# The convolution's four query channels during the projections, the other eight inside the attention heads

## The reference, cut to what matters

```python
def causal_conv(u, prev, w):                  # u: the 12 GDN channels, prompt: prev = 0
    full = jnp.concatenate([prev, u], axis=1)
    out = full[:, 0:L] * w[0]
    for i in range(1, CONV_W):                # CONV_W = 4
        out = out + full[:, i:i + L] * w[i]
    return out, full[:, L:]                   # the last three raw columns are an output
# gdn_mix: c = silu(out); q, k, v = split(c); q = l2norm(q) * 128**-0.5; k = l2norm(k); chunked delta rule
```

## Time and profile before

| | |
|---|---|
| time, median of 3 runs | 2565.94 us (2563.76 to 2568.59) |
| the profiled execution | 2564.64 us, of which its span is 2562.8 us |
| PE busy | 2469.6 us (96%) |
| weight load on PE busy | 2377.6 us (93%) |
| DVE busy | 1271.2 us (50%) |
| ACT busy | 563.2 us (22%) |
| POOL busy | 1692.2 us (66%) |
| mean granted clock of TensorE | 0.984 of full speed |

### The profile page before, as it was taken

The page is one execution under the profiler, slowest core; times in us unless marked ns, Lnnn a source line. Parts: engine busy times, 40 slices in busy tenths (PEclk is TensorE's granted clock), DMA queues, the critical chain, the costliest instruction groups (busy, mean ns, idle before and its releaser), DMA issues.

```text
span 2562.8 us, 52697 instructions
## 1 busy us (share of the span) xinstructions
PE 2469.6 (96%) x20031; PEld 2377.6 (93%) x20031; DVE 1271.2 (50%) x2204; ACT 563.2 (22%) x851; POOL 1692.2 (66%) x753
## 2 busy tenths in 40 slices
PE   7999998998799999999999999999999899999997
PEld 7999998997577899999999999999999799999996
DVE  4444435787533644443344443367767544444433
ACT  3222101003834222220022220122232211222101
POOL 5777776673523577777777787765555377777773
PEclk9999999998899999999999999999999999999998
DMA  4333333896466333333333333324333333333331
GB/s 120 92 92 95 100 91 77 273 313 193 139 199 190 103 91 90 90 99 91 106 91 90 91 99 90 89 86 124 121 94 119 102 95 88 92 95 90 100 92 56
DMA packets 472550, 291.20 MB, mean 114 GB/s; under 512 B 32945, under 2 KB 438571, under 8 KB 472430
## 3 DMA queue, kind: packets, MB, share of 16 engines
q1 hardware_dynamic: 415510, 235.83, 31.4%
q10 hardware_dynamic: 56928, 53.86, 6.5%
HBM read 273.50 MB, written 16.23 MB: 113 GB/s over the span
## 4 chain that ended last, share of the span: by engine, by line
PE 87%; DVE 7%; ACT 3%; POOL 1%; issue 1%; DMA 0%; ACTq 0%; SPq 0%; DVEq 0%; POOLq 0%
PE ACC L835 76%; PE ACC L1103 2%; PE ACC L1072 1%; POOL WLO L727 1%; PE ACC L1371 1%; PE ACC L1381 1%; DVE TB L2377 1%; DVE RMOL L2316 0%; PE ACC L1383 0%; POOL WHI L724 0%; DVE XL L1835 0%; DVE SSR L2294 0%; PE ACC L1282 0%; PE ACC L1168 0%; PE ACC L929 0%
## 5 line engine op out<-in xcount | busy, mean ns | idle before, releaser
L724 POOL TENSOR_TENSOR WHI<-RAW,ZERO 128x1024 fp32r<-128x1024 f32 (+1 forms) x341 | 691.5, 2028 | 635.7 <-PE ACC L835 593.1
L727 POOL TENSOR_TENSOR WLO<-RAW,WHI 128x1024 fp32r<-128x1024 f32 (+1 forms) x341 | 914.9, 2683 | 48.0
L835 PE MATMUL ACC<-XH,WHI 128*128 128x260 f32 x4032 | 821.9, 285 | 4.2 <-DVE XL L1835 1.9
L835 PE MATMUL ACC<-XH,WLO 128*128 128x260 f32 x4032 | 813.0, 283 | 0.0
L835 PE MATMUL ACC<-XL,WHI 128*128 128x260 f32 x4032 | 811.2, 283 | 0.0
L835 PEld LDWEIGHTS ACC<-XH,WHI 128*128 128x128 f32 x4032 | 624.2, 189 | 22.9 <-DVE PRJ L1922 6.1
L835 PEld LDWEIGHTS ACC<-XH,WLO 128*128 128x128 f32 x4032 | 622.0, 189 | 0.0
L835 PEld LDWEIGHTS ACC<-XL,WHI 128*128 128x128 f32 x4032 | 620.8, 188 | 0.0
L835 PE MATMUL ACC<-HH,WHI 128*128 128x260 f32 x1408 | 284.1, 283 | 1.1 <-POOL WLO L727 1.1
L835 PE MATMUL ACC<-HH,WLO 128*128 128x260 f32 x1408 | 283.1, 282 | 0.0
L835 PE MATMUL ACC<-HL,WHI 128*128 128x260 f32 x1408 | 282.5, 282 | 0.0
(11 more groups left out here) (403 smaller groups left out, 2368.7 us busy)
## 6 DMA issues: line engine op xcount, KB each, us to landing
RAW<-in_ffn_w_gu SPq DMA_DIRECT2D x176, 512.0 KB, 3.9
RAW<-in_ffn_w_down SPq DMA_DIRECT2D x64, 704.0 KB, 4.7
KPAGES<-in_cache_fox_k ACTq DMA_DIRECT2D x128, 256.0 KB, 4.3
VPAGES<-in_cache_fox_v SPq DMA_DIRECT2D x128, 256.0 KB, 3.7
RAW<-in_c_w_in SPq DMA_DIRECT2D x48, 512.0 KB, 3.9
RAW<-in_ab_w_in SPq DMA_DIRECT2D x28, 512.0 KB, 4.9
SSR<-in_state_ret_S ACTq DMA_DIRECT2D x8, 1024.0 KB, 6.8
out<-SSR ACTq DMA_DIRECT2D x8, 1024.0 KB, 5.6
```

The lines of the kernel that those rows point to most:

```text
L724: pool.tensor_tensor(WHI[:, slot, 0:nk, :], RAW[:, slot, 0:nk, :], ZERO[:, :].broadcast_to([P, nk, P]), ALU.add).then_inc(hi_split, 1)
L727: pool.tensor_tensor(WLO[:, slot, 0:nk, :], RAW[:, slot, 0:nk, :], WHI[:, slot, 0:nk, :].bitcast(F32), ALU.subtract).then_inc(split, 1)
L835: ins = pe.matmul(ACC[acc][:, n, 0:HALF], w[:, slot, k, :], a[:, k0 + k, n * HALF:(n + 1) * HALF], start=first and opens, stop=final and c ...
```

## The change: which channels are convolved where

Channels 0 to 3 are convolved during the projections. On ACT one step of `early_tap` (one shifted copy, or the scaling) follows each of the key loads 14 to 29; five buffers are taken in turn (SQ, SSQ, TB, TA and a new TAPX). The raw last columns are first copied to RAWTAIL, from which PE turns them. On POOL one addition (`early_add`) follows the split of each of the channels 18 to 27, and two more follow after those. Channels 4 to 11 go into the heads: 4, 5, 6 in head 0 at A, B and C; 7, 8, 9 in head 1, of which 7 and 8 both stand at B (A is empty) and 9 at C; 10 and 11 in head 2 at B and C (A is empty). None is left in the normalising.

```diff
+        EARLY_CONV, EARLY_BATCH = 4, 14
+        RAWTAIL = new("RAWTAIL", [P, EARLY_CONV, DEC + CONV_W - 1], area="ab")
+        EARLY_TAPS = (SQ, SSQ, TB, TA, at("TAPX", ...))
 POOL
-            split_phase("ab_in", KD, AB_CH // 4, 4, skip=1)
+            first_taps = AB_CONV + EARLY_CONV + 2
+            with pool.Fori(0, AB_CONV // 4) as i:
+                for s in range(4):
+                    split_unit(AB_UNIT + 4 * i + s, (AB_UNIT + s) % 2, KD, 2 * i + (AB_UNIT + s) // 2 + 1)
+
+            def early_add(n):
+                c, shift = n // (CONV_W - 1), n % (CONV_W - 1) + 1
+                pool.wait_ge(cv_tap, c + 1)
+                if shift > 1:
+                    await_step(pool, cv_pool, f"add{shift - 1}", c)
+                out = PRJ[:, AB_CONV + c, shift:SEQ]
+                cv_pool.done(pool.tensor_tensor(out, out, EARLY_TAPS[n % len(EARLY_TAPS)][:, shift:SEQ], ALU.add), f"add{shift}")
+
+            for f in range(AB_CONV, AB_CH):
+                split_unit(AB_UNIT + f, (AB_UNIT + f) % 2, KD, (AB_UNIT + f) // 2 + 1)
+                if f >= first_taps:
+                    early_add(f - first_taps)
+            for n in range(AB_CH - first_taps, EARLY_CONV * (CONV_W - 1)):
+                early_add(n)
...
             convolve_samples()
-            for c in range(CONV_CH):
+            for c in range(EARLY_CONV, CONV_CH):
                 convolve(c)
 PE
+            pe.wait_ge(cv_shifted, EARLY_CONV)
             for c in range(CONV_CH):
...
+                raw = RAWTAIL[:, c, :] if c < EARLY_CONV else PRJ[:, AB_CONV + c, SEQ - CONV_W + 1:TOK]
 ACT
+            def early_tap(c, k):
+                source = PRJ[:, AB_CONV + c, :]
+                if k == 0:
+                    act.wait_ge(tile_free, AB_TILE + AB_CONV + c + 5)
+                    act.activation(RAWTAIL[:, c, :], source[:, SEQ - CONV_W + 1:TOK], ACT.Copy)
+                if k < CONV_W - 1:
+                    shift, n = k + 1, (CONV_W - 1) * c + k
+                    if n == 3:
+                        act.wait_ge(gate_dve.sem, gate_dve.value("gcs"))
+                    if n >= len(EARLY_TAPS):
+                        reader = n - len(EARLY_TAPS)
+                        await_step(act, cv_pool, f"add{reader % (CONV_W - 1) + 1}", reader // (CONV_W - 1))
+                    ins = act.activation(EARLY_TAPS[n % len(EARLY_TAPS)][:, shift:SEQ], source[:, 0:SEQ - shift], ACT.Copy, scale=...)
...
+                else:
+                    act.wait_ge(cv_shifted, c + 1)
+                    act.activation(source[:, 0:SEQ], source[:, 0:SEQ], ACT.Copy, scale=...).then_inc(cv_tap, 1)
             for n in range(KEY_BATCHES):
                 load_keys(act, n % K_SLOTS, KBATCH * n, n)
+                if 0 <= n - EARLY_BATCH < EARLY_CONV * CONV_W:
+                    early_tap((n - EARLY_BATCH) // CONV_W, (n - EARLY_BATCH) % CONV_W)
...
             def conv_taps(c):
-                if c == 0:
+                if c == EARLY_CONV:
                     act.wait_ge(gp_pe.sem, gp_pe.value("tails"))
-                if c >= 2:
-                    await_step(act, cv_pool, "add3", c - 2)
+                await_step(act, cv_pool, "add3", max(c - 2, EARLY_CONV - 1))
...
                 if not last:
-                    conv_taps(3 * h)
+                    if h == 0:
+                        conv_taps(EARLY_CONV)
                     fox_turned(h, 2)
                     exponent(h + 1, 0)
                     exponent(h + 1, 1)
-                    conv_taps(3 * h + 1)
+                    if h == 1:
+                        conv_taps(EARLY_CONV + 3)
+                    conv_taps(EARLY_CONV + (1, 4, 6)[h])
                     fox_turned(h, 3)
                     exponent(h + 1, 2)
-                    conv_taps(3 * h + 2)
+                    conv_taps(EARLY_CONV + (2, 5, 7)[h])
...
-            for c in range(3 * (FOX_HEADS - 1), CONV_CH):
-                conv_taps(c)
```

More of the change, by code:

```diff
@@ L427, in trunk_program @@
         cs_pool = Steps(sem("cs_pool"), ["m0", "m1", "a1", "m2", "a2", "m3", "a3"])
+        EARLY_CONV, EARLY_BATCH = 4, 14
+        RAWTAIL = new("RAWTAIL", [P, EARLY_CONV, DEC + CONV_W - 1], area="ab")
+        EARLY_TAPS = (SQ, SSQ, TB, TA, at("TAPX", [P, SEQ], mo_at + PAGES_BYTES * K_SLOTS // 2 + 4 * CONV_CH * P))
         CONV_TILES = ((SQ, SSQ, TH), [at(f"TAP{n}", [P, SEQ], mo_at + 4 * (KD + FOX_HEADS) * TOK + 4 * SEQ * n) for n in range(3)])
@@ L1020, in _ @@
             pe.wait_ge(gp_act.sem, gp_act.value("prev"))
+            pe.wait_ge(cv_shifted, EARLY_CONV)
             for c in range(CONV_CH):
-                ins = pe.transpose(bank((2, 3, 6)[c // 4])[0:DEC + CONV_W - 1, (c % 4) * P:(c % 4 + 1) * P],
-                                   PRJ[:, AB_CONV + c, SEQ - CONV_W + 1:TOK], IDENT[:, :])
+                raw = RAWTAIL[:, c, :] if c < EARLY_CONV else PRJ[:, AB_CONV + c, SEQ - CONV_W + 1:TOK]
+                ins = pe.transpose(bank((2, 3, 6)[c // 4])[0:DEC + CONV_W - 1, (c % 4) * P:(c % 4 + 1) * P], raw, IDENT[:, :])
             gp_pe.done(ins, "tails")
@@ L1515, in _ @@
             act.wait_ge(pt_in, 48)
+            def early_tap(c, k):
[10 more added lines that the diff above has]
+                        await_step(act, cv_pool, f"add{reader % (CONV_W - 1) + 1}", reader // (CONV_W - 1))
+                    tap = PAR_CONV + CONV_CH * (CONV_W - 1 - shift) + c
+                    ins = act.activation(EARLY_TAPS[n % len(EARLY_TAPS)][:, shift:SEQ], source[:, 0:SEQ - shift], ACT.Copy, scale=PAR[:, tap:tap + 1])
+                    if k == CONV_W - 2:
+                        ins.then_inc(cv_shifted, 1)
+                else:
+                    act.wait_ge(cv_shifted, c + 1)
+                    tap = PAR_CONV + CONV_CH * (CONV_W - 1) + c
+                    act.activation(source[:, 0:SEQ], source[:, 0:SEQ], ACT.Copy, scale=PAR[:, tap:tap + 1]).then_inc(cv_tap, 1)
             for n in range(KEY_BATCHES):
                 load_keys(act, n % K_SLOTS, KBATCH * n, n)
+                if 0 <= n - EARLY_BATCH < EARLY_CONV * CONV_W:
+                    early_tap((n - EARLY_BATCH) // CONV_W, (n - EARLY_BATCH) % CONV_W)
             def channels(first, count):
@@ L1558, in _ @@
             fox_query(0)
+            await_step(act, cv_pool, "add3", EARLY_CONV - 2)
             fox_keys(0)
@@ L2009, in fox_value_tokens @@
                 await_step(dve, fa_pe, "vtok", h)
+                if h == 0:
+                    await_step(dve, cv_pool, "add3", EARLY_CONV - 2)
                 if h >= 2:
```

## The result

The changed kernel takes 2570.21 us, median of 19 runs (2564.64 to 2576.31), and the kernel before 2566.34 us (2562.85 to 2570.87, 19 runs): ratio 1.0014 [1.0007, 1.002], which is 3.6 us more (the medians themselves are 3.9 us apart), and inside the 0.2% that I had called "same". The interval excludes 1, so the sign is real. The profiled execution of the changed kernel has a span of 2567.8 us at a mean granted clock of 0.982; that of before 2562.8 us at 0.984.

A forecast was written before the change was run, and what follows sets the result against it. PE bounds the projections, ACT fills the heads, and PE's spreads and DVE's products carry the normalising. Terms 0 + 0 + 2.5 + 0 + 0 = +2.5 us on the 2565.94 us median gave 2568.4 us, range 2562.5 to 2572.0.

The forecast's parts named there:

- Head 1, +2.5 us: Head 1: A empty and 7, 8 both at B make ACT wait for PE, DVE and POOL; head ends 2.5 us later.
- Head 2, nothing given back: Head 2: the channel removed from A becomes ACT idle time, as key copy, PE and DVE set the exponential; 0 us.
- Projections, 0: Projections: four channels' work on ACT and POOL is hidden under PE; 0 us, bounds 0 to 1.5 us.
- The margin that I had worked out for late weights: Projections, channel 23's split: low part ends 567.49, PE needs it at 567.83, 0.34 us of margin.
- Head 0, 0: Head 0: A, B and C hold one channel each as before, no earlier channel pending; 0 us.
- Normalising, 0, and BEGE: Normalising: three channels off the chain leave, 0 us; BEGE's 0.80 us may shrink, bounds 0 to -0.7, absorbed waiting for PE.
- ACT's amount of work: Rival, heads: ACT's work sets the pace, nine channels becoming eight gives 2.6 us, 2563.3 us; chance 0.17.
- POOL's lateness: Rival, projections: loads 1.5 us late in three units, PE stands still 4 us, 2572.4 us; chance 0.11.
- The clock: Third rival, head 2: idle PE runs one more stretch at its lower clock, 2 us on top, 2570.4 us; chance 0.11.

The follow-up runs named there:

- Number 1: Changed kernel with channel 7 back at A of head 1, 8 at B and 9 at C: 2565.67 us against 2565.9, ratio 0.9999.
- number 8: The changed kernel run again, unaltered, for a second profile: 2569.45 us, ratio 1.0015 to the kernel before.
- Number 4: Changed kernel with channels 7, 8, 9 at A, B, C of head 1, 10 and 11 at A and B of head 2: 2566.12 us, ratio 1.0002.
- number 7: Changed kernel with all three channels of head 1 (7, 8, 9) at B, C empty: 2571.17 us, ratio 1.0022.
- 2: Changed kernel with 7 and 8 at B and C of head 1, 9 and 10 in head 2, 11 in the normalising: 2566.44 us, ratio 1.0002.
- number 5: The light version without the early convolution work of channels 0 to 3 (only the raw-column copy stays): 2562.36 us, ratio 0.9988.
- 3 second run: The light version made again on a different chip run: 2562.70 us against 2565.75, ratio 0.999.
- number 9: The light version with an addition of zero ahead of each of the twelve early additions on POOL: 2564.56 us, ratio 0.9997.
- 3 first run: The light version on its first chip run: 2560.38 us against 2565.9, ratio 0.9981.
- 6: The light version with channel 4 moved into ACT's wait for DVE's sample softmax, 5 and 6 at A and B of head 0: 2562.1 us, ratio 0.9984.
- the light version: Changed kernel with only 7 at B of head 1, 8 at B of head 2, and 9 to 11 in the normalising: 2560.38 and 2562.70 us.

## Why the prediction was right

The forecast of 2568.4 us lies 1.8 us below the median measured, 2570.21 us, which is just inside the forecast's own range of 2566.5 to 2570.3 us. That it fell inside and not beside is luck; the account rests on the places of the waits. Of the 1.8 us, 0.4 are the kernel before (2566.34 in 19 runs, 2565.94 in the three that I counted from), and the rest is the difference between the kernels. Step by step:

- *Head 1, +2.5 us.* Measured 2.7 and 2.5 us. The three waits forecast as 1.0, 1.0 and 0.5 us are 0.86, 1.06 and 0.42 us, ahead of the same three instructions and put down to the same engines. Number 1 shows that the empty place is the cause: with channel 7 back at A, and nothing else changed in the changed kernel, head and time are those of before.
- *Head 2, nothing given back.* Measured +0.3 us (13.63 against 13.38, both at a granted clock of 0.87). The mechanism is shown: ACT's lost 2.6 us of work stand in its waits. The size ahead of the copy of block 2 was off, 1.61 us for 2.3 forecast (1.97 in number 8), with the rest of it standing before the next exponential, where I had left the old wait at 0.69 us.
- *Projections, 0.* Right for the changed kernel. From the split of channel 18, where the early additions begin, to query copy 0 it takes 67.07 us, and 67.13 before; PE has no wait for WLO in this profile nor in number 8. The 0.5 us by which the projections end later stem from their start: over 445 to 480 us, before there is any early work, the granted clock is 0.89 against 0.91. The margin that I had worked out for late weights wasn't tried in this profile, as the weights came in time, but it was in others, and there it isn't always enough. In numbers 4, 7 and 2, where POOL waited 3.19, 1.40 and 1.56 us for late weights just before, PE waits 0.7, 0.7 and 0.3 us for the low part of WLO, and the same stretch takes 67.98, 67.95 and 67.59 us. Number 4:

```profile
549.65 0.48 PE L856 MATMUL ACC<-XH,WHI 128*128 128x260 f32 x2 [0.68 <-POOL WLO L730]
```

  POOL's waits for weights of 3.4 us before and of up to 3.1 us in number 5, both without early additions, cost PE nothing (67.13 and 67.06 us). So the early additions are hidden, except for up to 0.9 us in some executions with late weights, three of the nine profiles that have one addition per unit. That is inside the bounds of 0 to 1.5 us.
- *Head 0, 0.* It is 0.3 us out. From query copy 0 to query copy 1 before takes 13.87 us and number 5 13.90; with early work seven profiles (after and numbers 1, 3 second run, 4, 7, 8, 9) take 14.18 or 14.19, so that this small cost goes with the early work. The other three (2, 3 first run, 6) take 15.8 us, with a stretch of PE at its lower clock level in it. ACT's key copy of head 0 starts later after PE's signal: 

```profile
600.82 0.60 ACT L1577 ACTIVATE TA<-ACC 128x512 f32<-128x512 f32 x1 [1.72 <-PE ACC L991]
```

```profile
600.32 0.60 ACT L1575 ACTIVATE TA<-ACC 128x512 f32<-128x512 f32 x1 [1.43 <-PE ACC L991]
```

  (after, and number 5, which has the same waits in its program). Why ACT needs these 0.3 us more isn't settled.
- *Normalising, 0, and BEGE.* BEGE lost its 0.6 us as the Trainium skill's rule on who holds whom at the SBUF has it ("SBUF — State Buffer", section "Who interferes with whom"): 0.17 us with POOL silent. The first GAM step behind it comes 2.87 us after the last product of the spreads, and 3.22 before, so 0.35 us are gained there. Nothing of it is left at KBE: from the last product to the first copy of KBE it takes 7.63 and 7.75 us in after and number 8, and 7.61 and 7.72 in the two profiles of the light version, where BEGE takes 0.80 us again. One thing I passed over in the rows: BEGE began late before, since it waited 1.09 us for ACT's EGC copy, which stood behind channel 11. That wait is gone too, and is as well covered by PE.
- *The remaining 1.1 us* (3.6 measured against 2.5) are within what 19 runs of each can tell (1.8 to 5.1); 0.3 of them are the copy in head 0 and some 0.2 head 2.

Of the rivals, ACT's amount of work is refuted: its idle time in heads 1 and 2 grew from 0.9 us (0.10 and 0.79) to 5.9 (2.44 and 3.48), by 5.0 us where the rival allowed 2.6. POOL's lateness is small and rare at one addition per unit (0.3 to 0.7 us, three profiles of nine) and plain at two; the rival's 4 us came in none. The clock is open in part. PE's granted clock in head 2 is 0.87 in before and after alike, and the third rival's extra stretch didn't come; but in number 1 head 2, with the same two channels at B and C, lasts 12.12 us instead of 13.6 without the slow stretch, and number 7 paid for one in head 1. It varies between executions where the work is the same. The record of the runs gives a check, as each execution has its mean granted clock. At 0.984 the changed kernel's executions have a median of 2568.1 us (8 of them, both runs) and those of before 2564.5 us (33, beside numbers 1 to 9); at 0.982 it is 2569.9 (9) against 2566.9 us (31). So 3.0 to 3.6 us remain where the clock is the same, to the rounding of 0.001, and the difference doesn't rest on the clock; that a smaller part of it is clock I can't exclude.

What the change missed stands in number 3. It emptied the place where three channels cost nothing, beside the normalising, and kept five in heads 1 and 2, where the light version has two. At full clock the second and third channel at B and C of head 1 cost 2.6 us and more each; in head 2 the second costs 0.9 us (12.12 in number 1 against 11.2), as PE's own length takes over.

## What to carry to other kernels

Count a piece of filler work by the wait that it stands in, not by its length: the same three channels made a head of 12.6 or 15.3 us, both at full clock, according to whether one of them stood in the wait for PE's turned block. Work to be hidden goes first to stretches where the engine is off the chain (here the projections and the normalising), then one piece into each wait of the busy stretch, and what is left over is the cost. Before removing work from a place, look at what the engine waits for just behind it; if there is a wait already, the removal gives little (0.6 us of 2.6 in head 1). And compare stages of two profiles only where their granted clock is the same: here a slow stretch moved a head by 1.1 to 1.6 us.

## What the hardware showed beside this

- An addition of 128 x 511 on POOL takes 1.27 to 1.30 us with two full operands and 1.04 us when one is a broadcast zero (number 9). I had taken them as equal.
- ACT's activation table was changed at 681.43, during the wait of 9.12 us that the copy of EGC then ended at 691.83:

```profile
691.83 0.22 ACT L1687 ACTIVATE EGC<-RT 128x16 f32<-128x16 f32 x1 [9.12 <-DVE PRJ L2137]
```

  The load was issued ahead of the wait, so it cost nothing there.
- Two profiles of the same kernel differ by 4.0 us in span (2567.8 and 2563.8) with waits in head 1 that agree within 0.16 us. Past the last head 3.6 us of it arise: 2.6 ahead of the last square root, where 16 products of 128 x 512 (L1094) took 3.60 us in one and 1.90 in the other, and 0.9 behind it, where PE's spreads have a median of 636 ns in one and 481 ns in the other.
